# Two mixed attention and expert layers on one core: a new order of expert steps, and results added one step later

## The chip, the cores and the metric

One Trainium2 chip, of which the program uses 1 core. The metric is the device time of one launch in microseconds. The time before is the median of three runs, 1272.5 us (1272.12, 1276.44 and 1272.5).

## The reference, cut to what matters

Two layers run over 256 tokens of width 1024 (128 context tokens and 128 latent ones). Each layer is a block of three kinds of attention, an output projection `w_out`, and then a layer of 64 experts, six for each token, plus one shared expert. The change touches the expert layer only:

```python
def swiglu(x, wg, wu, wd):
    return (silu(x @ wg) * (x @ wu)) @ wd            # 1024 -> 256 -> 1024

def moe_ffn(h, p):                                   # 256 tokens
    xf = h.reshape(T, D)
    top_idx, top_w = route(xf, p['router_w'], p['router_bias'])   # 6 experts of 64
    ...
    yb = lax.map(expert_block, (xb, block_e))        # swiglu with the weights of expert e
    routed = segment_sum(yb[dest] * w_s[:, None], tok_s, num_segments=T)
    shared = swiglu(xf, p['sh_w_gate'], p['sh_w_up'], p['sh_w_down'])
    return (routed + shared).reshape(B, N, D)
```

All weights are f32. Each expert has three matrices (gate, up, down) of 1024 KB, so a layer reads 192 of them from memory once.

How many tokens an expert gets depends on the data. With the inputs of this case, the busiest experts among the 58 that are ranked (below) have 74, 47, 41, 41, 39, 39, 38, 35, 35, 34, 34, 32, 32, 29, ... tokens in layer 0 and 67, 47, 47, 40, 39, 37, 36, 35, 33, 33, 33, 32, 32, 30, ... in layer 1. The six experts that are not ranked have at most 33.

## The kernel before, in words

**Units and steps.** An expert's work is a unit. Units 0 to 5 are the experts 0 to 5 (static: their weights can be fetched before the router has run); the other 58 experts are ranked by their token counts once routing is known, and unit u is the expert of that rank. A step works on 128 slots of tokens: kind S is one unit with 128 slots, D is two units of 64, Q is four units of 32. `ORDER` (line 46) gives each step's kind and first unit. It has 21 steps, numbered from 0. After step 9 (`LOOP = 10`) comes a step in a loop, a D that works on two more units (62 and 63, which are the experts of ranks 18 and 19, ahead of the lighter ones) and, if an expert has more tokens than its unit has slots, on further ones: the loop runs `again` times, at least once. So a layer has 22 steps when nothing overflows. `AGAIN` is the first unit of the loop.

**A step on TensorE** (`step`, with the helpers inside it):
- gate products (L1387, with b = 6) and up products (L1387, b = 7), 64 each at most, from the gathered tokens `xg`;
- the gather for the next step (L1330, twice 16 products: tokens `h2` times the 0/1 matrix `pick`), and between its halves four transposes (L1400, L1402);
- down products (L1420, two halves of 8);
- adding (L1352, 16 products): the step's result `ysb`, spread back to the tokens by the weights `sa`, is added to `xview` in PSUM. It comes right behind the down products whose result it needs.

In the last step there is no gather, and between gate and up stand five products on constants (L1364, warm-up). Its down loads come as halves.

VectorE builds `pick` (`choose`) and `pickw` (`weigh`), copies the first half of each gather and each down result; ScalarE copies the second halves. A semaphore count of a gather is G, of a step J; with an extra gather behind the loop (the loop's last pass has gathered for a pass that does not come) G is J plus a correction.

**Which unit is which.** `slots_by_expert` (L1267, four transposes) and `slots_by_unit` (L1274, four products) turn the positions and weights of the tokens from the order of experts into that of units. Before, they stand inside step 0, and step 1's up products wait for the result (`units`), though step 1 itself is static.

**The weights' way in.** Every weight load is issued by SyncE, in one queue, in the order of the table `LOADS`: loads n = 0 to 191 a layer, 1024 KB each (and one for the shared expert's down matrix). First the 18 loads of the three static steps, then, step by step, gate, up, down. On chip they go into 19 chunks: 12 of a ring, and `attn`, `attn_w`, two of `spare`, `mixed`, `ht` and `wide`, which serve other work in the attention part. `chunk_places` says which load goes to which chunk and which earlier load it replaces. SyncE waits until the products that use the earlier load are through: for a gate load's chunk until that step's gate products (`gl`), up (`gu`), down (`y1`). Since the queue is in order, a load that waits holds back all behind it.

The first loads of the dynamic steps, before: load 18 waits for the router (`plan`), 19 and 20 for step 0's gate products, 21 and 22 for its up, 23 and 24 for its down; 25 and 26 for step 1's gate, 27 and 28 for its up, 29 and 30 for its down. Loads 18 to 29 are those of the step with units 18 to 21 (step 2), 30 to 41 of that with 22 to 25 (step 4). Load 31 waits for step 2's gate products.

During the output projection the ring chunks 6 to 11 hold `w_out`, in two slots of 6144 columns of which it uses 4096. All of chunks 6 to 11 are handed out only once `w_out` has been used (`y_mm`, L1159).

```python
                    if p == 6:
                        sp.wait_ge(S["y_mm"], KD * (l + 1))
...
                                sp.wait_ge(S[used_by[part]], x + ((x + 15) >> 4) + (done + LOOP - 1))
...
                pe.wait_ge(S["xga"], done + (LOOP + l + 1))
                pe.wait_ge(S["xgb"], done + (LOOP + l + 1))
                for _ in gather(done + (LOOP + l + 1)):
                    pass
```

## Time and profile before

| | |
|---|---|
| median of three runs | 1272.5 us (1272.12 to 1276.44) |
| profiled execution, its own time | 1273.4 us |
| its span | 1271.6 us |
| mean granted TensorE clock | 0.987 |
| TensorE busy | 1209.9 us (95%) |
| VectorE busy | 310.4 us (24%) |
| ScalarE busy | 192.9 us (15%) |
| DMA traffic | 495.00 MB, mean 389 GB/s |
| expert steps of layer 0 | from about 182 to 640 us |
| expert steps of layer 1 | from about 800 to 1258 us |

The rows further down come from this one profiled execution. Times are microseconds from the start of the span. Engines: PE is TensorE, PEld its weight loads, DVE VectorE, ACT ScalarE, SP SyncE, and a q behind a name is that engine's sequencer, which issues DMAs. A line number is that of the kernel before. "out<-in" names the buffers; in a line with a wait, `<-` names what ended it. PEclk is the granted TensorE clock as a share of full speed, and the DMA share is the mean busy share of the 16 DMA engines, which the view can put a little above 1.

### The profile page before, as it was taken

What the parts mean: (1) busy time and instruction counts of PE and PEld (TensorE: products, weight loads), DVE (VectorE), ACT (ScalarE), POOL (GpSimd) and SP (SyncE); (2) the same over time, 40 slices, a digit from 0 to 9 for tenths busy, and PEclk for the clock granted to TensorE, in tenths of its full rate; (3) what the DMA queues carried; (4) which work ended last, traced back from release to release, by engine and by line L of the source; (5) the groups of instructions that cost most, each with busy time, mean ns of one, the idle gap of its engine ahead of it and who ended that gap; (6) DMA issues with size and microseconds to landing.
All of it is one profiled execution on the core that took longest, in us unless ns stands there. A gap on an engine that the chain in (4) does not pass through costs nothing.

```text
span 1271.6 us, 22858 instructions
## 1 busy us (share of the span) xinstructions
PE 1209.9 (95%) x9511; PEld 800.5 (63%) x9511; DVE 310.4 (24%) x883; ACT 192.9 (15%) x471; POOL 37.7 (3%) x73
## 2 busy tenths in 40 slices
PE   8999999999999999988899999999999999999795
PEld 4445876666577767655554567766566776775563
DVE  2057341213111111111130764221311121111112
ACT  1125221100111011100010442011011010110011
POOL 2210000000000000000020100000000000000000
PEclk9999999999999999998999999999999999999899
DMA  9999998999999999999996896999999999999995
GB/s 369 389 388 404 407 368 344 383 419 420 421 421 421 420 420 420 421 399 420 409 372 248 328 369 248 350 358 420 420 421 421 420 420 421 421 421 408 421 421 203
DMA packets 86630, 495.00 MB, mean 389 GB/s; under 512 B 11948, under 2 KB 18016, under 8 KB 33024
## 3 DMA queue, kind: packets, MB, share of 16 engines
q1 hardware_dynamic: 83744, 488.38, 94.7%
q0 software_dynamic: 2240, 4.64, 1.1%
q8 instruction: 76, 1.25, 0.4%
q10 hardware_dynamic: 544, 0.52, 0.1%
q14 instruction: 26, 0.21, 0.0%
HBM read 491.20 MB, written 2.50 MB: 388 GB/s over the span
## 4 chain that ended last, share of the span: by engine, by line
PE 58%; issue 24%; DMA 9%; DVE 4%; SPq 3%; ACT 1%; POOL 0%; POOLq 0%; ACTq 0%; DVEq 0%
PE ps L1387 14%; PE ps L931 7%; PE ps L1330 7%; PE ps L1420 6%; PE ps L1352 6%; PE ps L1159 4%; DMA ring<-in_exp_w_up 4%; DMA ring<-in_exp_w_down 4%; PE ps L898 3%; PE ps L1283 2%; SPq L655 2%; SPq L650 1%; PE ps L1116 1%; DMA ring<-in_w_ada 1%; DMA mixed<-in_exp_w_down 1%
## 5 line engine op out<-in xcount | busy, mean ns | idle before, releaser
L1387 PE MATMUL ps<-ring,kt_buf 128*32 128x256 f32 (+2 forms) x3200 | 307.9, 390 | 24.6 <-DMA ring<-in_exp_w_up 15.5
L1387 PEld LDWEIGHTS ps<-ring,kt_buf 128*32 128x32 f32 (+2 forms) x3200 | 190.0, 123 | 121.0 <-issue 45.4
L1330 PE MATMUL ps<-kt_buf,attn 128*128 128x128 f32 x1472 | 185.9, 280 | 1.8 <-DVE kt_buf L2016 1.8
L1330 PEld LDWEIGHTS ps<-kt_buf,attn 128*128 128x128 f32 x1472 | 174.9, 194 | 17.0 <-issue 14.3
L1352 PE MATMUL ps<-kt_buf 128*128 128x256 f32 x704 | 163.8, 385 | 3.2 <-DVE kt_buf L2134 1.8
L1352 PEld LDWEIGHTS ps<-kt_buf 128*128 128x128 f32 x704 | 130.3, 190 | 56.2 <-issue 22.7
L1420 PE MATMUL ps<-ring,kt_buf 128*32 128x512 f32 (+1 forms) x544 | 135.3, 611 | 2.7 <-DMA ring<-in_exp_w_down 2.7
L931 PE MATMUL ps<-ring,ht 128*128 128x456 f32 x256 | 98.9, 547 | 0.6 <-DVE ht L1694 0.6
L2122 DVE SCALAR_TENSOR_TENSOR kt_buf<-kt_buf,ps 128x256 f32<-128x256 f32 x44 | 18.5, 421 | 325.3 <-ACT kt_buf L1619 325.3
L931 PEld LDWEIGHTS ps<-ring,ht 128*128 128x128 f32 x256 | 48.3, 190 | 50.4 <-issue 48.2
L1621 ACT ACTIVATE kt_buf<-ps 128x512 f32<-128x512 f32 x44 | 26.3, 597 | 288.0 <-PE ps L1402 288.0
L2134 DVE COPY kt_buf<-ps 128x512 f32<-128x512 f32 x44 | 30.4, 692 | 141.0 <-PE ps L1420 141.0
L1159 PE MATMUL ps<-ht,ring 128*128 128x256 f32 x256 | 58.7, 382 | 0.0
L1420 PEld LDWEIGHTS ps<-ring,kt_buf 128*32 128x32 f32 (+1 forms) x544 | 34.6, 120 | 37.3 <-issue 34.8
L1619 ACT ACTIVATE kt_buf<-ps 128x256 f32<-128x256 f32 x44 | 16.9, 385 | 270.5 <-PE ps L1387 270.5
L2125 DVE TENSOR_TENSOR kt_buf<-kt_buf,ps 128x256 f32<-128x256 f32 x44 | 18.5, 421 | 153.9 <-PE ps L1387 153.9
L1420 PE MATMUL ps<-attn_w,kt_buf 128*32 128x512 f32 (+2 forms) x112 | 52.2, 597 | 1.9 <-ACT kt_buf L1621 1.4
L2051 DVE COPY kt_buf<-ps 128x512 f32<-128x512 f32 x46 | 31.8, 691 | 86.2 <-PE ps L1330 86.2
L1387 PE MATMUL ps<-spare,kt_buf 128*32 128x256 f32 (+1 forms) x448 | 52.6, 389 | 0.0
L1420 PE MATMUL ps<-attn,kt_buf 128*32 128x512 f32 (+2 forms) x112 | 51.9, 597 | 0.5 <-DMA spare<-in_exp_w_down 0.5
L1159 PEld LDWEIGHTS ps<-ht,ring 128*128 128x128 f32 x256 | 47.4, 190 | 6.1 <-issue 0.3
L1630 ACT ACTIVATE kt_buf<-ps 128x512 f32<-128x512 f32 x44 | 26.3, 597 | 147.7 <-PE ps L1420 147.7
(307 smaller groups left out, 1158.2 us busy)
## 6 DMA issues: line engine op xcount, KB each, us to landing
ring<-in_exp_w_up SPq DMA_DIRECT2D x104, 1024.0 KB, 22.7
ring<-in_exp_w_gate SPq DMA_DIRECT2D x96, 1024.0 KB, 21.0
ring<-in_exp_w_down SPq DMA_DIRECT2D x68, 1024.0 KB, 19.6
ring<-in_w_ada SPq DMA_DIRECT2D x10, 3072.0 KB, 14.1
spare<-in_exp_w_up SPq DMA_DIRECT2D x16, 1024.0 KB, 26.8
spare<-in_exp_w_down SPq DMA_DIRECT2D x16, 1024.0 KB, 26.7
attn<-in_exp_w_down SPq DMA_DIRECT2D x14, 1024.0 KB, 21.3
spare<-in_exp_w_gate SPq DMA_DIRECT2D x12, 1024.0 KB, 8.9
```

What stands on the lines that cost most here:

```text
L655: sp.dma_start(down_of(c)[:, :, h * 512:(h + 1) * 512], I["exp_w_down"][l, e, :, h * 512:(h + 1) * 512].rearrange("(p k) n -> p k n", p=P) ...
L898: last = pe.matmul(ps[32 * q:32 * q + 32, 7, :], csilu[:, k, :], ring[:, slots[l][ent], o:o + 512], start=(k in (0, apart)), stop=(k in (a ...
L931: return pe.matmul(ps[:, 4 * t + n, 0:NZ], ht[:, k, t * T:(t + 1) * T], rows_of(l, i)[:, k - WIN_K[i][0], o:o + NZ], start=(k == 0), stop= ...
L1159: last = pe.matmul(ps[:, Y_BANK[c % 4], (c // 4) * 256:(c // 4) * 256 + 256], w, ht[:, k, :], start=(k == 0), stop=(k == KD - 1))
L1330: last = pe.matmul(ps[:, 4 + b, (c % 4) * P:(c % 4 + 1) * P], h2[:, t, c * P:(c + 1) * P], pick[:, t, :], start=(t == 0), stop=(t == NG - 1))
L1352: last = pe.matmul(xview[:, c, :], ysb[:, c * P:(c + 1) * P], sa[:, 0:NG * T], start=(i == 0 and c % 2 == 0), stop=True, skip_group_check= ...
L1387: last = pe.matmul(ps[w * e:w * (e + 1), b, 0:DE], xg[:, k, w * e:w * (e + 1)], half_of(chunk_of(l, load_of(part, i, e)))[:, k, :], start= ...
L1420: last = pe.matmul(ps[w * e:w * (e + 1), 4 + b, :], sa[:, 256 + k * P + w * e:256 + k * P + w * (e + 1)], down_of(chunk_of(l, load_of("dow ...
L1621: act.activation(sa[:], ps[:, 7, :], ACT.Copy).then_inc(S["sa"], 1)
L1630: act.activation(ysb[:, 512:1024], ps[:, 5, :], ACT.Copy).then_inc(S["yb"], 1)
L2051: dve.tensor_copy(xg[:, 0:4, :].rearrange("p a b -> p (a b)"), ps[:, 4, :]).then_inc(S["xga"], 1)
L2134: dve.tensor_copy(ysb[:, 0:512], ps[:, 4, :]).then_inc(S["ya"], 1)
```

## The change

1. **Adding is put off by a step.** The adding products for step J - 1 now stand in step J, behind its up products; in the last step between the gate products and the warm-up. The last step's own result is added at its end as before. Step 0 adds nothing, step 1 opens the accumulation.
2. **Early assignment.** `slots_by_expert` and `slots_by_unit` move ahead of step 0, into the gathers for it. They use the PSUM banks 0 and 1 now, and ScalarE and not VectorE copies `by_expert`.
3. **Two fixed chunks beside w_out.** Chunks 8 and 11, the third ones of the two slots, which `w_out` does not use, are handed out before the rest of 6 to 11, so two loads more are issued before the wait for `y_mm`.
4. **Useful last gather of the loop.** VectorE writes the first units of step 10 behind the loop's last units, so the last gather of the loop is step 10's. The gather behind the loop is gone, and G equals J everywhere.
5. **20 steps and the loop's** in place of 21 and the loop's, and a new order. A new kind T has three units (64, 32, 32 slots). One D and one S step are gone and one T step has come; there are 11 Q steps as before. The first dynamic step, Q18, is step 1. The loop's units 62 and 63 are now the ranks 16 and 17, and units 16 and 17, with T's 32 slots, hold the ranks 18 and 19; unit 7, which had 128 slots, has 64.
6. Room for 34 further units in place of 32, and constants that nothing reads are dropped.

```diff
-FEW = {"S": 1, "D": 2, "Q": 4}
-SLOTS = {"S": 128, "D": 64, "Q": 32}
+SLOTS = {"S": (128,), "D": (64, 64), "T": (64, 32, 32), "Q": (32, 32, 32, 32)}
+FEW = {kind: len(slots) for kind, slots in SLOTS.items()}
-ORDER = (("D", 0), ("D", 2), ("Q", 18), ("D", 4), ("Q", 22), ("Q", 26), ("D", 8), ("Q", 30), ("S", 6), ("Q", 34),
-         ("Q", 38), ("D", 10), ("Q", 42), ("D", 12), ("S", 7), ("Q", 46), ("D", 14), ("Q", 50), ("Q", 54), ("D", 16), ("Q", 58))
+ORDER = (("D", 0), ("Q", 18), ("D", 2), ("Q", 22), ("D", 4), ("Q", 26), ("Q", 30), ("S", 6), ("Q", 34), ("D", 7),
+         ("D", 9), ("Q", 38), ("Q", 42), ("Q", 46), ("Q", 50), ("Q", 54), ("D", 11), ("T", 15), ("D", 13), ("Q", 58))
...
+BESIDE_OUT = (8, 11)
...
-    opened = [SPARE_C, SPARE_C + 1] + list(range(6)) + [ATTN_C, ATTN_W_C, MIXED_C] + list(range(6, RCH)) + [HT_C, WIDE_C]
+    opened = [SPARE_C, SPARE_C + 1] + list(range(6)) + [ATTN_C, ATTN_W_C, MIXED_C] + list(BESIDE_OUT) \
+        + [c for c in range(6, RCH) if c not in BESIDE_OUT] + [HT_C, WIDE_C]
...
-                                sp.wait_ge(S[used_by[part]], x + ((x + 15) >> 4) + (done + LOOP - 1))
+                                sp.wait_ge(S[used_by[part]], x + ((x + 31) >> 5) + (done + LOOP - 1))
...
-                    def add(b):
+                    def add(b, of, signal=False):
 
-                        pe.wait_ge(S["ya" if b == 0 else "yb"], J + 1)
+                        pe.wait_ge(S["ya" if b == 0 else "yb"], of)
                         for c in range(4 * b, 4 * b + 4):
                             last = pe.matmul(xview[:, c, :], ysb[:, c * P:(c + 1) * P], sa[:, 0:NG * T],
-                                             start=(i == 0 and c % 2 == 0), stop=True, skip_group_check=True)
+                                             start=(i == 1 and c % 2 == 0), stop=True, skip_group_check=True)
...
+                    def add_step_before():
+
+                        add(0, J)
+                        add(1, J)
...
                         if end and b == 7:
+                            add_step_before()
 
                             for _ in range(WARM_LAST):
                                 pe.matmul(ps[:, 7, :], ident, tbl[:, 0:512], start=True, stop=True)
...
                         last.then_inc(S[signal], 1)
+                    if i and not end:
+                        add_step_before()
                     if i == SHARED[2]:
                         shared_down()
...
-                    if i == 0:
-                        slots_by_expert()
...
                         if end:
-                            add(b)
-                    if not end:
-                        add(0)
-                        add(1)
+                            add(b, J + 1, signal=True)
+                    if i == 0:
+                        pe.wait_ge(S["units"], l + 1)
 
                 pe.wait_ge(S["h2"], 2 * l + 2)
-                g = gather(done + l)
+                g = gather(done)
                 next(g)
                 next(g)
                 order_experts()
+                slots_by_expert()
                 next(g)
                 list_experts()
+                slots_by_unit()
...
-                pe.wait_ge(S["xga"], done + (LOOP + l + 1))
-                pe.wait_ge(S["xgb"], done + (LOOP + l + 1))
-                for _ in gather(done + (LOOP + l + 1)):
-                    pass
                 for i in range(LOOP, STEPS):
-                    step(done + i, done + (i + l + 1), ORDER[i][0], i, end=(i == STEPS - 1))
+                    step(done + i, ORDER[i][0], i, end=(i == STEPS - 1))
...
                 again = dve.value_load(xpairs[0:1, 0:1], min_val=1, max_val=XP_MAX)
+                after = bass.ds(2 * again + AGAIN, FEW["D"])
+                first = slice(ORDER[LOOP][1], ORDER[LOOP][1] + FEW["D"])
+                dve.tensor_copy(posu[:, :, after], posu[:, :, first])
+                then(dve.tensor_copy(wu[:, :, after], wu[:, :, first]))
```

How instructions stand on an engine is shown in the next fences: a line number, the operation, out<-in and the shape, how many in a row, and which semaphore the first one waits for.

SyncE in layer 0, from the fourth gate load of the step with units 18 to 21 on, before (a `TENSOR_LOAD` of `xexp` reads the expert's number for a gate load):

```order
L735 TENSOR_LOAD xexp [waits s_gu]
L735 ISA x2
L650 ISA
L650 DMA ring<-in_exp_w_gate 128x2048
L650 DMA ring<-in_exp_w_up 128x2048
L650 DMA ring<-in_exp_w_up 128x2048 [waits s_y1]
L650 DMA ring<-in_exp_w_up 128x2048
L650 DMA ring<-in_exp_w_up 128x2048 [waits s_gl]
L650 DMA ring<-in_exp_w_down 128x2048
L650 DMA attn<-in_exp_w_down 128x2048 [waits s_gu]
L650 DMA attn_w<-in_exp_w_down 128x2048
L650 DMA ring<-in_exp_w_down 128x2048 [waits s_y1]
```

The same place after:

```order
L650 DMA ring<-in_exp_w_gate 128x2048
L650 DMA ring<-in_exp_w_up 128x2048
L650 DMA ring<-in_exp_w_up 128x2048 [waits s_y1]
L650 DMA ring<-in_exp_w_up 128x2048
L650 DMA ring<-in_exp_w_up 128x2048 [waits s_gl]
L650 DMA spare<-in_exp_w_down 128x2048 x2
L650 DMA ring<-in_exp_w_down 128x2048 [waits s_gu]
L650 DMA ring<-in_exp_w_down 128x2048
L735 TENSOR_LOAD xexp [waits s_gu]
```

The rows are loads 21 to 29, then 30. Before, the wait for `s_gl` ahead of load 25 is for the gate products of step 1, which is static and for which these loads are not. After, step 1 is the step that these loads are for: load 25 (its fourth up matrix) waits for its own gate products, 26 and 27 likewise, 28 and 29 for its own up products, and load 32 for its own down products.

TensorE in layer 0 from the end of step 0's second gather half to the next gate products, before:

```order
L1330 MATMUL ps<-kt_buf,attn 128x128 x8
L1420 MATMUL ps<-ring,kt_buf 64x512 x4
L1274 MATMUL ps<-attn_w,ada_sb 128x64 x4
L1420 MATMUL ps<-ring,kt_buf 64x512 x4
L1352 MATMUL ps<-kt_buf 128x256 x8
L1387 MATMUL ps<-ring,kt_buf 64x256 x16
```

After, what stands ahead of step 0's gate products (from the order of experts on):

```order
L1267 MATMUL ps<-tbl,mixed 64x128 x2
L1267 MATMUL ps<-tbl,kvg 64x128 x2
L1330 MATMUL ps<-kt_buf,attn 128x128 x8
L1260 MATMUL ps<-attn_w,tbl 1x64
L1274 MATMUL ps<-attn_w,ada_sb 128x64 x4
L1391 MATMUL ps<-spare,kt_buf 64x256 x16
```

After, step 1 from its up products to its first down products:

```order
L1391 MATMUL ps<-ring,kt_buf 32x256 x33
L1352 MATMUL ps<-kt_buf 128x256 x8
L1330 MATMUL ps<-kt_buf,attn 128x128 x8
L1406 MATMUL ps<-tbl,kt_buf 128x128 x2
L1408 MATMUL ps<-tbl,kt_buf 128x128 x2
L1330 MATMUL ps<-kt_buf,attn 128x128 x8
L1424 MATMUL ps<-spare,kt_buf 32x512 x2
```

The products L1267 and L1274 have left step 0, step 0's down products are followed by step 1's gate products, and adding (L1352) stands between step 1's up products and the gather.

TensorE around the last step's gate products, before:

```order
L1402 MATMUL ps<-tbl,kt_buf 128x128 x2
L1330 MATMUL ps<-kt_buf,attn 128x128 x8
L1420 MATMUL ps<-ring,kt_buf 64x512 x8
L1352 MATMUL ps<-kt_buf 128x256 x8
L1387 MATMUL ps<-ring,kt_buf 32x256 x32
L1364 MATMUL ps<-tbl 128x512 x5
L1387 MATMUL ps<-ring,kt_buf 32x256 x3
```

After:

```order
L1408 MATMUL ps<-tbl,kt_buf 128x128 x2
L1330 MATMUL ps<-kt_buf,attn 128x128 x8
L1424 MATMUL ps<-ring,kt_buf 64x512 x8
L1391 MATMUL ps<-ring,kt_buf 32x256 x32
L1352 MATMUL ps<-kt_buf 128x256 x8
L1370 MATMUL ps<-tbl 128x512 x5
L1391 MATMUL ps<-ring,kt_buf 32x256 x3
```

Adding has moved from ahead of the last gate products to between them and the warm-up products (L1364 before, L1370 after).

## Rows read from the trace of the kernel before

**Rows 1.** The page: slices of traffic (each 31.8 us), and its DMA issues (median us to landing)

```profile
GB/s 369 389 388 404 407 368 344 383 419 420 421 421 421 420 420 420 421 399 420 409 372 248 328 369 248 350 358 420 420 421 421 420 420 421 421 421 408 421 421 203
...
ring<-in_exp_w_up SPq DMA_DIRECT2D x104, 1024.0 KB, 22.7
```

**Rows 2.** Windows: stretch, us, busy PE, PEld, DVE, ACT, POOL, PEclk, DMA share, GB/s

```profile
182.00:240.00 58.00, 58.00 (x496) 38.86 (x496) 14.09 (x43) 7.13 (x13) 0.00 (x0) 1.00 0.90 348
240.00:546.00 306.00, 303.66 (x2573) 207.65 (x2573) 54.74 (x129) 34.78 (x65) 0.00 (x0) 1.00 1.01 420
546.00:640.00 94.00, 78.62 (x739) 48.59 (x738) 12.03 (x28) 7.51 (x14) 0.00 (x0) 0.95 1.00 409
776.00:784.00 8.00, 8.00 (x44) 7.17 (x44) 3.17 (x12) 0.83 (x2) 0.00 (x0) 1.00 0.00 0
802.00:857.00 55.00, 55.00 (x471) 37.08 (x468) 12.18 (x35) 6.53 (x12) 0.00 (x0) 1.00 0.89 343
```

**Rows 3.** Waits of SyncE's DMA queue: waited for, total us, times, longest

```profile
SPq L561 <- PE ps L1387: 263.3, 53, 23.4
...
SPq L650 <- PE ps L1159: 33.5, 2, 22.1
```

**Rows 4.** Chain of waits, 182 to 240 us: start, us, what

```profile
182.34 7.06 PE ps L1387 x64
...
191.84 0.44 PE ps L1267 x4
...
195.93 1.03 PE ps L1274 x8
...
198.83 3.65 PE ps L1352 x16
202.48 7.06 PE ps L1387 x64
209.53 1.98 PE ps L1330 x16
...
213.75 3.58 PE ps L1420 x16
...
220.99 7.04 PE ps L1387 x128
```

**Rows 5.** Timeline of SyncE's DMA issues: load 23, and load 31

```profile
199.00 0.33 SPq L650 DMA_DIRECT2D ring<-in_exp_w_up  x1
...
225.42 0.34 SPq L650 DMA_DIRECT2D ring<-in_exp_w_gate  x1
```

**Rows 6.** DMA issues (median us to landing): loads 23/24, 31, and 23/24 of layer 1

```profile
ring<-in_exp_w_up SPq DMA_DIRECT2D x2, 1024.0 KB, 6.3
...
ring<-in_exp_w_gate SPq DMA_DIRECT2D x1, 1024.0 KB, 4.8
...
ring<-in_exp_w_up SPq DMA_DIRECT2D x2, 1024.0 KB, 8.5
```

**Rows 7.** Windows for line L1387 alone: PE, PEld, PEclk, DMA share, GB/s

```profile
575.00:581.00 6.00, 0.00 (x0) 0.00 (x0) 0.90 1.01 416
581.00:588.00 7.00, 6.31 (x64) 3.18 (x64) 0.60 1.02 425
1200.00:1206.00 6.00, 5.35 (x64) 3.30 (x64) 0.72 1.02 426
```

**Rows 8.** Timeline of TensorE, layer 1, last steps: start, us, operation [idle before]

```profile
1210.28 0.59 PE L1420 MATMUL ps<-attn,kt_buf 128*32 128x512 f32 x1 [0.48 <-DMA spare<-in_exp_w_down]
...
1236.02 3.66 PE L1387 MATMUL ps<-ring,kt_buf 128*32 128x256 f32 x64
1239.61 4.56 PE L1364 MATMUL ps<-tbl 128*128 128x512 f32 x10
...
1246.50 0.42 PE L1387 MATMUL ps<-ring,kt_buf 128*32 128x256 f32 x3 [2.33 <-DMA attn<-in_exp_w_up]
...
1257.14 0.59 PE L1420 MATMUL ps<-attn_w,kt_buf 128*32 128x512 f32 x1 [0.15 <-DMA mixed<-in_exp_w_down]
```

More of the change, by code:

```diff
@@ L1334, in gather, with step @@
                         yield
-                def step(J, G, kind, i, extra=None, end=False):
-                    w = SLOTS[kind]
+                def step(J, kind, i, extra=None, end=False):
+                    slots_of = [slice(sum(SLOTS[kind][:e]), sum(SLOTS[kind][:e + 1])) for e in range(FEW[kind])]
                     def wait_for(part):
@@ L1612, in copy_second, with step @@
                         .then_inc(S["xgb"], 1)
-                def step(J, G, shared=None, end=False):
+                def step(J, shared=None, end=False):
                     act.wait_ge(S["gl"], J + 1)
@@ L1641, in _ @@
                         shared_tanh(SHARED.index(i))
-                        step(done + i, done + (i + l), shared=SHARED.index(i))
+                        step(done + i, shared=SHARED.index(i))
                     else:
-                        step(done + i, done + (i + l))
+                        step(done + i)
                 act.wait_ge(S["more"], l + 1)
@@ new lines, in of_units @@
+                def of_units(table, u, few):
+                    return table[:, :, u:u + few] if isinstance(u, int) else table[:, :, bass.ds(u, few)]
+                def choose(kind, u):
+                    for first, few, w, at in equal_slots(kind):
+                        last = dve.tensor_tensor(pick[:, :, at].rearrange("p t (e s) -> p t e s", e=few),
+                                                 tbl[:, C_SLOT:C_SLOT + w].unsqueeze(1).unsqueeze(1)
+                                                 .to_broadcast([P, NG, few, w]),
+                                                 of_units(posu, u + first, few).unsqueeze(3)
+                                                 .to_broadcast([P, NG, few, w]), ALU.is_equal)
+                    last.then_inc(S["sel"], 1)
@@ L2030, in _ @@
+                    last.then_inc(S["sw"], 1)
                 choose(*ORDER[0])
```

137 lines of the change are left out of this document (58 added, 79 removed).

## The prediction

> **What bounds the kernel now.** I read the page's slices first, then the stage windows, then SP's waits, then the chain of waits through the first expert steps, and last the timelines of the last step. In the slices the traffic stands at 420 GB/s through the middle of both expert phases [rows 1], and the stage windows put a number on it: 420 GB/s at a DMA share of 1.01 for 306 us of layer 0, against 348 GB/s and 0.90 in the 58 us ahead of it, and 343 GB/s and 0.89 at the same place of layer 1 [rows 2]. One load is 1024 KB; at 420 GB/s that is 2.50 us, and the 192 expert loads and the shared one of a layer are 193 x 2.50 = 482 us. TensorE looks as full as the queue (58.00 of 58.00 us, 303.66 of 306.00), but in the last 94 us it is busy for 78.62 us only while the traffic stays at 409 [rows 2]. So TensorE runs ahead and then waits at the end of each layer for data. The queue is the bound, and it loses time only where it has nothing to do: at the start of the expert phase, where 18 loads lie ready and each further one waits until TensorE has used up a chunk (SP waits 263.3 us in 53 waits for the gate and up products, [rows 3]).
>
> I split the change by what it can do to two things: the moment from which the queue never runs dry again, and what stands between the last landing and the end.
>
> **The step that goes, and the extra gather: no gain of their own.** A step is 220.99 - 202.48 = 18.51 us of TensorE whatever it holds: gate and up 7.06, gather and transposes 213.75 - 209.53 = 4.22, down 3.58, adding 3.65 [rows 4]. One step a layer goes (18.5 us) and the gather behind the loop, twice 1.98. These 22.5 us lie in the 306 us in which the queue is saturated, and the bytes stay the same. The cover is the load that is still on its way: 22.7 us from issue to landing in the median [rows 1]. If that cover were not there (TensorE the true bound), it would be a gain of 22.5 us a layer, which is a rival below. Whether a unit overflows depends on the counts: the first expert on 32 slots is now that of rank 18 (the thirteenth of the ranked ones), and with 32 tokens in both layers it just fits, so the loop still runs once, as before.
>
> **Two loads ahead of w_out's end: nothing.** In layer 1 the queue is idle at 776 to 784 (0 GB/s, [rows 2]) while SP waits for the w_out products (33.5 us in two waits, [rows 3]). Two loads, 5 us, now fill this. But they are of step 2, the queue has caught up with all 18 before step 0 is over, and it then runs dry anyway waiting for chunks. The bounds: nothing, or 5 us a layer if the queue never ran dry behind it; the share of 0.89 behind it [rows 2] decides for nothing.
>
> **The new start: Q18 as step 1.** Layer 0 of the trace, moved by hand:
> - The products that assign slots (0.44 and 1.03 us, [rows 4]) now stand ahead of step 0's gate and not inside step 0: the gate starts 1.47 later, the down products still end at 198.83. With adding put off, step 1's gate starts there and ends at 202.4.
> - Loads 23 and 24 wait for step 0's down products as before: issued at 199.00, landed after 6.3 us in the mean of the two [rows 5, 6], the second at 206.7.
> - Load 25 now waits for step 1's own gate, is behind them in the queue and lands at 206.7 + 2.5 = 209.2. Step 1's up products need it: TensorE stands idle for 6.8 us, where it had no wait at all.
> - After such a wait, 6 us in this trace, the granted clock was 0.60 over the window of the next 64 products and they took 6.31 us instead of the 3.66 that they take at full clock [rows 7, 8]; that is a stretch at 1.2 of 2.4 GHz. So up ends at 215.5, and not 212.8.
> - Adding 3.65, gather and transposes 4.22, down 3.58: step 1 ends at 227.0. Loads 28 and 29, issued at 215.8, land at 220.6 and 223.1 (4.8 us for a load into an empty queue, [rows 6]) and are just in time.
> - Load 32 waits for these down products. Load 31 of the trace was issued 0.9 behind its release (the gate half of the products that start at 220.99 ends at 224.5, the issue is at 225.42, [rows 4, 5]); with the same 0.9 it is 227.9, landing 232.7. It is the last that starts into a dry queue.
> - Before, the last dry one is load 31, issued at 225.42 [rows 5], landing 230.2; load 32 behind it lands at 232.7 at the earliest. So the start gives 0 in layer 0.
> - In layer 1 the two loads behind step 0's down products took 8.5 us and not 6.3 [rows 6]. Before, this had slack; now load 25 hangs on it, so 2.2 us are lost there. I take half, 1.1, since the stretch behind it before was not free of the same delay.
> Bounds for the start: with the full clock in the up products 2.65 a layer better, that is 5.3 - 1.1 = 4.2 us gained; at worst, with the full 2.2 and as much again in layer 0, 4.4 us lost. I take 1 us lost, since the 6.31 comes from a wait of the same length.
>
> The Trainium skill (TensorE: Matmul & The Clock Gate, "HAM oscillation — how this bites in real kernels") says that waits for DMA send the array back to its slow clock, so that each burst behind one starts cold. The trace agrees (6.31 against 3.66, [rows 7, 8]); without the rule the start would come out 5.3 us better over two layers. The same skill (DMA: Bandwidth & Descriptors, "Anatomy of one DMA — SWDGE (gpsimd) path") fits one DMA as 2.0 us plus bytes over 436 GB/s, an estimate of 4.4 us for ours; the trace has 4.8 [rows 6] and decides; by the page the start would be 0.4 a layer better.
>
> **The middle.** Steps 9, the loop's and 10 are now three pair steps in a row: TensorE needs 18.5 for each, the queue 15.0, so 10.5 us of the queue's lead go. Of the 22.7 us [rows 1] 12 are left, over the 4.8 that a load needs: nothing.
>
> **The last step.** Adding for the step before moves from ahead of the last gate to behind it, ahead of the five warm-up products. Layer 1, before: down 1210.28 (after a wait for its load), two addings, one pair step, gate 1236.02, warm-up 1239.61 for 4.56, ends 1244.17, and the up products wait 2.33 more, until 1246.50, for their load [rows 8]. The step with that down is now T15. Its up loads land three loads (7.5 us) ahead of its down load, at 1202.8, and between the two TensorE must now do up 3.53, adding 3.65 and gather 4.22, 11.4 us: down starts at 1214.2, 3.9 late. Then down 3.58, gate and up 7.06, adding 3.65, gather 4.22, down 3.58: 1236.3; gate 3.6, adding 3.65, warm-up 4.56: 1248.1. The up load is there at 1246.5, so up starts 1.6 late. The last down half waits for its own load by only 0.15 us at 1257.14 [rows 8], so 1.45 of this shows at the end of the layer. With layer 0 the same: 3 us lost. Bounds: 0 (the clock or the copies give it back) and 3.9 x 2 = 7.8 us (nothing hides it).
>
> **The sum**: start 1 lost, last steps 3 lost, step, gather, early loads and middle 0: 4 us slower, less 1.5 us for small gaps in the traffic of the last 94 us, which a TensorE that uses up its chunks earlier can close (409 GB/s against 420 there is 2.5 us a layer at most, [rows 2]; of both layers' 5 I take a third). Net +2.5. The profiled execution took 1273.4 us (span 1271.6), so 1275.9 there; the runs' median is 0.9 lower: 1275.
>
> **The rivals.**
> - *The early four-expert step pays.* If the clock does not fall in step 1 and the last step's lateness is absorbed, the start's 4.2 and the gaps' 2.5 remain: 1266. For it: half the price rests on one wait's clock. Against: 6.31 us after 6 us idle, and 5.35 after a shorter one at 1200 us [rows 7].
> - *TensorE is the bound*, as its busy time and SP's 263.3 us of waits for it suggest: 22.5 us a layer, 1228. Against: the queue stands at its top rate all that time.
> - *The starved start (slower).* Step 1 is the place: four gates, four ups and four downs with 19 chunks held by steps 0, 2 and 4. If loads 23 to 25 take 8.5 us in both layers and the down products wait too for load 29, each layer's dry queue lasts 3 us longer, and every later pair step runs 3 us nearer to it; with the last steps at 3.9 each the sum is 6 + 7.8 less 3 = 11 slower: 1283. It decides from a step 1 that ends over 3 us later than 227.0.
> - *A unit overflows*, because a near tie in routing falls the other way on the chip: one more pass of the loop, 6 loads of 2.50, 15 us a layer: 1290 to 1305.
>
> **How the numbers follow.** Forecast 0.44; early step pays 0.28, half of it beyond 0.5%; TensorE the bound 0.07; starved start 0.18, most of it beyond 0.5%; overflow 0.03. A measurement of this kernel tells 0.5% (6.4 us) from no change. Faster: 0.14 + 0.07 and a little of the forecast, 0.23. Slower: 0.14 + 0.03, 0.17. Same: 0.60. The range holds the forecast and most of the cases on both sides: 1262 to 1284. The forecast's own is 1270 to 1280.
>
> **What would show it.** Right, if in the new trace step 1's up products start after 6 to 7 us of idle time named after a DMA, at a clock of about a half; the queue's last dry moment is at 226 to 229; the traffic is 420 through the middle; TensorE's idle time in a layer's expert steps grows by some 22 us, what it no longer has to do; and the last up products start with no idle time ahead of them, behind the warm-up. Wrong, if the steps stay free of waits to the end and the middle gets shorter, if step 1 has no wait, or if the loop runs twice.

## The result and the profile after

The changed kernel takes 1312.7 us in the median of four runs (1311.19 to 1316.54), the kernel before 1272.3 us beside it: a ratio of 1.0317, 95% interval 1.030 to 1.0335. It is 40 us slower; 1275 us were forecast, with a range up to 1284. The profiled execution took 1311.2 us, its span is 1309.4 us, 37.8 us more than before. In both traces layer 0 ends where the products of line 875 begin: 642.8 us before, 661.7 us after. That is 18.9 us, and the second layer loses the other half.

The page of the changed kernel, the slices of traffic and the DMA issues (as in [rows 1]):

```profile
GB/s 370 390 384 410 408 360 332 418 419 420 421 395 405 373 421 421 421 420 422 410 195 242 334 371 290 321 352 419 420 422 415 410 374 409 420 422 420 421 405 42
...
ring<-in_exp_w_up SPq DMA_DIRECT2D x96, 1024.0 KB, 17.3
```

The windows of the changed kernel, with the columns of [rows 2], a window in the middle (427 to 450 us), and then the T step and the pair step D13 by themselves:

```profile
182.00:240.00 58.00, 48.87 (x439) 33.77 (x439) 9.79 (x26) 5.24 (x10) 0.00 (x0) 0.94 0.88 337
240.00:546.00 306.00, 278.55 (x2491) 184.90 (x2489) 51.39 (x132) 31.51 (x60) 0.00 (x0) 0.96 1.00 411
427.00:450.00 23.00, 23.00 (x231) 15.63 (x228) 3.52 (x8) 2.18 (x4) 0.00 (x0) 1.00 0.87 353
546.00:640.00 94.00, 91.62 (x653) 53.53 (x654) 11.36 (x25) 8.71 (x16) 0.00 (x0) 0.97 1.02 417
583.30:616.90 33.60, 33.60 (x174) 13.73 (x171) 2.89 (x6) 2.18 (x4) 0.00 (x0) 1.00 1.01 421
616.90:635.20 18.30, 18.30 (x134) 12.71 (x132) 2.56 (x5) 2.18 (x4) 0.00 (x0) 1.00 1.02 406
```

The middle window of the kernel before:

```profile
427.00:450.00 23.00, 23.00 (x177) 15.02 (x178) 4.30 (x10) 3.28 (x6) 0.00 (x0) 1.00 1.01 419
```

Two things stand out. In the middle of layer 0 the queue is not full any more: 353 GB/s for 23 us in which TensorE is busy all the time (the kernel before has 419 there). And at the end TensorE, which waited for 15 us of the 94 before, is busy for 91.62 of them: the T step (the one with units 15 to 17) takes 33.6 us of it, the pair step behind it (D13, units 13 and 14) 18.3, at the same full clock.

The timeline of TensorE in the changed kernel, step 1 and then the shared expert's products ahead of step 6 (start, us, operation, idle time before):

```profile
198.79 0.38 PE L1391 MATMUL ps<-wide,kt_buf 128*32 128x256 f32 x1 [1.51 <-DMA ring<-in_exp_w_gate]
...
210.07 5.19 PE L1391 MATMUL ps<-ring,kt_buf 128*32 128x256 f32 x64 [7.62 <-DMA ring<-in_exp_w_up]
...
307.60 9.39 PE L1283 MATMUL ps<-heads,ht 128*128 128x512 f32 x16 [4.91 <-DVE ht L1694]
```

The same products in the kernel before:

```profile
299.57 7.10 PE L1283 MATMUL ps<-heads,ht 128*128 128x512 f32 x16 [1.26 <-DVE ht L1694]
```

The start came as forecast: 7.6 us idle ahead of step 1's up products. The last line was not in the forecast: TensorE waits 4.9 us for VectorE there and not 1.3, and the products take 2.3 us longer, at a granted clock of 0.75 in their window and not 1.00.

The chain of waits of the changed kernel at the end of layer 0 (start, us, what):

```profile
554.96 13.39 DMA ring<-in_exp_w_up
...
568.48 3.67 PE ps L1391 x32
...
579.83 3.58 PE ps L1424 x16
583.42 17.96 PE ps L1391 x96
601.37 3.65 PE ps L1352 x16
...
609.05 7.94 PE ps L1424 x24
616.99 7.06 PE ps L1391 x64
...
635.30 3.59 PE ps L1391 x64
638.89 3.65 PE ps L1352 x16
642.54 4.29 PE ps L1370 x10
646.84 3.63 PE ps L1391 x64
```

From 568.48 to 650.47 the chain is TensorE alone, 82 us. The last half load of the layer was issued at 626.99 before the change and at 630.78 after it, and landed 11.2 and 11.3 us later:

```profile
626.99 1.03 SPq L655 DMA_DIRECT2D mixed<-in_exp_w_down  x1
mixed<-in_exp_w_down SPq DMA_DIRECT2D x1, 512.0 KB, 11.2
...
630.78 1.04 SPq L655 DMA_DIRECT2D mixed<-in_exp_w_down  x1
mixed<-in_exp_w_down SPq DMA_DIRECT2D x1, 512.0 KB, 11.3
```

So the last landing was at 638.2 with the layer's end 4.6 us behind it, and is now at 642.0 with the end 19.6 us behind it. Of the 18.9 us, the last landing is 3.8 later, and the end stands 15 further behind it. In the chain the T step's gate and up products are 17.96 us where a pair step's are 7.06, and its down products 7.94 where they are 3.58: 15.3 us too many.

TensorE's weight loads in the T step (same columns):

```profile
583.77 0.14 PEld L1391 LDWEIGHTS ps<-ring,kt_buf 128*32 128x32 f32 x4 [0.39 <-issue]
584.33 0.19 PEld L1391 LDWEIGHTS ps<-ring,kt_buf 128*64 128x64 f32 x2 [0.41 <-issue]
584.90 0.14 PEld L1391 LDWEIGHTS ps<-ring,kt_buf 128*32 128x32 f32 x4 [0.39 <-issue]
```

A product leaves two records here (one k, an eighth of the 1024 inputs, is four products in eight records in a Q step). Each k of the T step runs as two groups, the 64-slot product and the two of 32 slots, 0.565 us apart, so 1.13 us for a k. A pair or four products of one width take 0.441 us (7.06 us for the 16 k of gate and up). Nothing of the narrow group lies beside the wide one.

### The profile page after: what moved, and what is told of

The parts are those of the page before. It is cut to its first block, busy times and chain, and to the rows that moved or that the text cites. A ratio compares the mean times of both kernels' runs of the same rounds, so it can differ in the third digit from the quotient of the medians.

```text
span 1309.4 us, 22476 instructions
## 1 busy us (share of the span) xinstructions
PE 1203.0 (92%) x9343; PEld 772.5 (59%) x9343; DVE 301.5 (23%) x871; ACT 188.5 (14%) x463; POOL 37.8 (3%) x73
## 3 DMA queue, kind: packets, MB, share of 16 engines
HBM read 491.17 MB, written 2.50 MB: 377 GB/s over the span
## 4 chain that ended last, share of the span: by engine, by line
PE 60%; issue 24%; DMA 8%; DVE 4%; SPq 2%; ACT 1%; POOL 0%; POOLq 0%; ACTq 0%; DVEq 0%
PE ps L1391 15%; PE ps L931 7%; PE ps L1352 7%; PE ps L1330 7%; PE ps L1424 7%; PE ps L1159 4%; DMA ring<-in_exp_w_up 4%; PE ps L898 3%; PE ps L1283 3%; DMA attn<-in_exp_w_up 2%; SPq L650 1%; DMA ring<-in_exp_w_gate 1%; PE ps L1116 1%; DMA ring<-in_w_ada 1%; PE ps L1141 1%
## 5 line engine op out<-in xcount | busy, mean ns | idle before, releaser
L1391 PE MATMUL ps<-ring,kt_buf 128*32 128x256 f32 (+2 forms) x3040 | 320.7, 405 | 27.6 <-DMA ring<-in_exp_w_up 16.7
L1391 PEld LDWEIGHTS ps<-ring,kt_buf 128*32 128x32 f32 (+2 forms) x3040 | 171.7, 124 | 131.4 <-issue 80.3
L1330 PE MATMUL ps<-kt_buf,attn 128*128 128x128 f32 x1344 | 164.1, 275 | 1.8 <-DVE kt_buf L2025 1.8
L1330 PEld LDWEIGHTS ps<-kt_buf,attn 128*128 128x128 f32 x1344 | 160.1, 192 | 4.7 <-ACT attn L1604 1.0
L1352 PE MATMUL ps<-kt_buf 128*128 128x256 f32 x672 | 156.6, 386 | 3.2 <-DVE kt_buf L2138 1.8
L1352 PEld LDWEIGHTS ps<-kt_buf 128*128 128x128 f32 x672 | 124.2, 190 | 37.3 <-issue 15.3
L1391 PE MATMUL ps<-spare,kt_buf 128*32 128x256 f32 (+2 forms) x512 | 84.3, 391 | 17.3 <-DMA ring<-in_exp_w_up 12.6
L1391 PEld LDWEIGHTS ps<-spare,kt_buf 128*32 128x32 f32 (+2 forms) x512 | 45.4, 124 | 40.0 <-issue 27.4
L1391 PE MATMUL ps<-mixed,kt_buf 128*32 128x256 f32 (+1 forms) x160 | 43.2, 432 | 18.1 <-DMA ring<-in_exp_w_up 12.6
L1391 PE MATMUL ps<-attn,kt_buf 128*32 128x256 f32 (+1 forms) x192 | 49.5, 402 | 0.0
```

Of the source, the lines that this page charges most:

```text
L1330: last = pe.matmul(ps[:, 4 + b, (c % 4) * P:(c % 4 + 1) * P], h2[:, t, c * P:(c + 1) * P], pick[:, t, :], start=(t == 0), stop=(t == NG - 1))
L1352: last = pe.matmul(xview[:, c, :], ysb[:, c * P:(c + 1) * P], sa[:, 0:NG * T], start=(i == 1 and c % 2 == 0), stop=True, skip_group_check= ...
L1391: last = pe.matmul(ps[slots_of[e], b, 0:DE], xg[:, k, slots_of[e]], half_of(chunk_of(l, load_of(part, i, e)))[:, k, :], start=(k == 0), st ...
```

## The experiments

All ran beside the kernel before, in four sets: t_four to t_four_cover, defer_only to tail, no_warm to no_cover, and the last three. The medians of the kernel before were 1273.2, 1272.3, 1273.0 and 1271.2 us in these sets, so 1 or 2 us between kernels of different sets mean nothing; the ratios, with 95% intervals, compare better.

**t_four.** The T step's 64-slot unit as two products of 32 slots from the same chunk.

```diff
...
+                    if kind == "T":
+                        slots_of = [(0, slice(0, 32)), (0, slice(32, 64)), (1, slice(64, 96)), (2, slice(96, 128))]
...
-                            for e in range(FEW[kind]):
-                                last = pe.matmul(ps[slots_of[e], b, 0:DE], xg[:, k, slots_of[e]],
+                            for e, at in slots_of:
+                                last = pe.matmul(ps[at, b, 0:DE], xg[:, k, at],
```

> The changed kernel (1312.7 us), with the three-unit step's 64-slot unit worked as two products of 32 slots from the same chunk, so that the step issues four products of 32 at a time like a Q step. Theory A (the mixed widths 64, 32, 32 make the T step slow, and the end of each layer hangs on TensorE): gate and up of the T step fall from 18.1 to about 7.1 us, down from 7.9 to 3.6, the step from 33.6 to 18.3; 15.3 us a layer, 1282 us. Rival B (the loss comes from the order of the last steps and from a queue that ran dry in the middle; the T step's length is hidden behind loads): within 5 us of the changed kernel, 1308 to 1312. Rival C (the granted clock, 0.97 against 0.987, is the cause): the T step stays long.

Measured: 1289.7 us (ratio 1.0131, 1.010 to 1.0162), 23 us less. The timeline of its T step:

```profile
584.78 3.66 PE L1393 MATMUL ps<-ring,kt_buf 128*32 128x256 f32 x64
590.71 0.65 PE L1393 MATMUL ps<-ring,kt_buf 128*32 128x256 f32 x3 [2.27 <-DMA attn<-in_exp_w_up]
```

The window of its up products, for their line alone (columns as in [rows 7]):

```profile
590.71:595.92 5.21, 5.21 (x64) 2.71 (x64) 0.68 1.00 415
```

The gate products take 3.66 us. Behind them TensorE now waits 2.27 us for a load, and the up products take 5.21 us at a clock of 0.68. With the 3.66 of full clock, that is 3.8 us lost in layer 0; in layer 1 the wait is 1.33 us and the clock full. So 5.1 of the 7.6 us that are missing between the 23 that came back and 30.6 are seen, and the rest is open. Rivals B and C fall: same order, same clock (0.966), 23 us less.

**t_apart.** The T step's products with the 64-slot unit first for all k, then the two others; the down products likewise.

```diff
+                        runs = ((0,), (1, 2)) if kind == "T" else (range(FEW[kind]),)
-                        for k in range(KD):
+                        for k, few in [(k, few) for few in runs for k in range(KD)]:
...
-                            for e in range(FEW[kind]):
+                            for e in few:
```

> The changed kernel (1312.7 us), with the T step's products in two runs: the 64-slot unit for all k first, then the two 32-slot units for all k. If the T step loses both by the lack of overlap between the two widths and by each switch of width (now at each k): gate and up fall from 18.1 to 14.2 us (4 runs of 8 at 0.445 each), down from 7.9 to 7.3, so 4.5 us a layer and 1304 us. If only the lack of overlap counts and a switch is free: no change, 1312. If only the alternation is at fault and the widths overlap: 18.1 to 7.1 and 1282.

Measured: 1306.2 us (1.0256, 1.0239 to 1.0274), 6.5 us less. The gate and up products of the T step as a window for their line alone (columns as in [rows 7]), first of this kernel:

```profile
585.41:599.78 14.37, 14.37 (x96) 7.72 (x95) 1.00 1.02 423
```

and of the changed kernel:

```profile
583.25:601.37 18.12, 18.12 (x96) 5.30 (x95) 1.00 1.01 421
```

32 groups at 0.441 us are 14.1 us, nearly all that is left when each width runs by itself. So two things make up the loss. Each k has two groups and not one, 7.1 us. And a change of width costs time: the edit takes away 28 of the 31 changes and 3.75 us (18.12 less 14.37), 0.13 us each, about what the start times say (0.565 less 0.441). That the widths don't overlap while they alternate is read from those start times; t_apart keeps them apart and can't show it.

**cover.** The adding for step 5 ahead of the shared products of step 6.

```diff
+                    if i == SHARED[0]:
+                        add_step_before()
+                        shared_gate_up(0)
                     pe.wait_ge(S["xga"], J + 1)
...
-                    if i and not end:
+                    if i and not end and i != SHARED[0]:
                         add_step_before()
```

> The changed kernel (1312.7 us), with the adding for step 5 put back ahead of step 6's shared gate and up products (elsewhere it stays put off). Before the change it filled the time in which VectorE prepares the shared expert's input; after, TensorE waits 4.9 us there (1.3 before) and the shared products take 9.4 us at a lower clock (7.1 before). Theory D (this wait puts TensorE behind, and the queue runs dry at 429 to 448 us for some 5 us): wait and slow clock go, 5.9 us of TensorE a layer, and with the dry queue up to 5 us a layer of the total: 1302 to 1307. Rival (the wait is hidden since the queue is full): 1311 to 1313.

Measured: 1303.8 us (1.0235, 1.0211 to 1.0259), 9 us less, within theory D's range. TensorE waits 1.26 us ahead of the shared products again, and they take 7.11 us. The window from 427 to 450 us carries more:

```profile
311.19 7.11 PE L1283 MATMUL ps<-heads,ht 128*128 128x512 f32 x16 [1.26 <-DVE ht L1697]
...
427.00:450.00 23.00, 23.00 (x224) 16.13 (x221) 3.31 (x7) 2.17 (x4) 0.00 (x0) 1.00 0.98 399
```

399 GB/s against 353, with no other edit: TensorE's lateness had kept chunks from the queue.

**t_four_cover.** Both edits.

> Both: the T step as four products of 32, and the adding for step 5 ahead of the shared products. If the two causes add (15.3 and some 5 us a layer): 1272, as before the change. If the T step alone sets the end: 1282, as with that edit alone. If, with the T step mended, the last landing sets the end: between these, 1275 to 1280, and the last up products of a layer wait for a load again.

Measured: 1277.3 us (1.0035, 1.0026 to 1.0045): 35 us less than the changed kernel, 12.3 less than t_four. The time is that of the third expectation, but its sign is missing: the last up products of layer 0 start with no wait for a load. Layer 0 ends at 642.75 us, as before the change (642.81).

**defer_only.** The kernel before, with the adding put off and nothing else.

```diff
+                            add(0, J)
+                            add(1, J)
 
                             for _ in range(WARM_LAST):
...
+                    if i and not end:
+                        add(0, J)
+                        add(1, J)
...
-                    if not end:
-                        add(0)
-                        add(1)
```

> The kernel before (1272.5 us) with one part of the change alone: the adding of a step's result put off into the next step (in the last step ahead of the warm-up products), and at the gather behind the loop a wait for the copies that the adding used to wait for. Theory D (put off, the adding no longer covers the time in which the shared expert's input is prepared; TensorE waits about 5 us and the clock falls): the wait ahead of the shared products of step 6 grows from 1.3 to about 5 us, these take 9.4 and not 7.1 us, but as the queue does not run dry in the middle of this kernel, only the last step's 1.5 us a layer show: 1275 us. If TensorE sets the middle here too: 6 us a layer more, 1284. Rival (putting off is free or a gain): 1272 or less.

Measured: 1273.5 us (1.0013, 1.0004 to 1.0023). The wait ahead of the shared products is 4.91 us and they take 9.62, and yet the kernel loses only 0.5 to 3 us by the interval. So the wait is hidden here.

**old_order.** The changed kernel with the table of steps of before. (Its step 10 is a Q step, while the loop's last gather is laid out for a pair step. So of step 10's four experts one gets its tokens, one gets those of another expert, and two get none. The instructions are those of a Q step in number and shape.)

> The changed kernel (1312.7 us) with the order of the steps of before (21 steps, no T step) and all else of the change kept. Theory (the order with its T step and its run of pair steps made the loss): within 5 us of before, 1272 to 1277. Rival (adding put off, early assignment or the loop's useful gather cost much of it): over 1285.

Measured: 1269.5 us (0.9977, 0.9967 to 0.9987). The order, with the T step in it, makes the whole loss: without it 1312.7 becomes 1269.5 us.

**old_start.** t_four_cover with the first steps D0, D2, Q18, D4, Q22.

> The changed kernel with the T step as four products and the adding for step 5 ahead of the shared products (1277.3 us), and with the first five steps in the order of before (D0, D2, Q18, D4, Q22). Theory E (the four-unit step as step 1 starves TensorE for 6 to 7 us in each layer and leaves the queue dry 2 us longer): last dry load lands at about 230 and not 232 us, step 1 has no wait, 2 to 3 us a layer less: 1272. Rival (the early four-unit step is no loss, since the end of a layer hangs on TensorE's chain behind the last four-unit step but one): 1277 to 1280, the wait only comes later.

Measured: 1270.8 us (0.9984, 0.9974 to 0.9994), 6.5 us less than t_four_cover. The last load of the start that lands behind a dry queue is load 29 at 223.3 us and not load 32 at 232.0. I had expected 230. With the adding put off, step 2's gate products come sooner, and load 31, which waits for them, is issued at 220.25 and not 225.42 [rows 5]; the queue is not dry then. defer_only issues it at 222.15, so most of this is the put-off adding, which the early Q step had hidden.

```profile
220.25 0.34 SPq L650 DMA_DIRECT2D ring<-in_exp_w_gate  x1
```

**tail.** t_four_cover with the end Q46, D11, Q50, T15, Q54, D13, Q58.

> The changed kernel with the T step as four products and the adding for step 5 ahead of the shared products (1277.3 us), and with the small steps at the end dealt out between the four-unit steps: ... Q46, D11, Q50, T15, Q54, D13, Q58. Theory F (with D11, T15, D13 in a row TensorE is 1 to 3 us late at the end, 10.6 to 11.5 us behind the last landing and more): the last up products wait for their load again, and the layer ends about 10 us behind the last landing: 1 to 2 us a layer less, 1274. Rival (the queue sets the end and each layer ends as before): 1277.

Measured: 1277.9 us (1.0053, 1.0036 to 1.007), no change from t_four_cover. Theory F falls: where the T step costs no more than a pair step, dealing out the small steps brings nothing.

**no_warm.** old_start with `WARM_LAST = 0`.

> The kernel old_start (1270.8 us) without the five warm-up products ahead of the last up products. Its trace has no wait ahead of these products: the chain adding (3.7), warm-up (4.5), up is later than the load, and layer 0 ends 11.8 us behind its last landing, where the kernel before ended 10.0 us behind it. Theory G (TensorE's chain sets the end of each layer there): 1.8 us a layer less, until the last landing sets the end: 1267. Rival (without the warm-up the products behind run at half clock): 1271 or more.

Measured: 1269.4 us (0.9972, 0.9959 to 0.9985), 1.4 us under old_start's value, with intervals that overlap, so no gain is shown. In the timeline the last up products wait for their load once more:

```profile
624.73 0.42 PE L1396 MATMUL ps<-ring,kt_buf 128*32 128x256 f32 x3 [3.01 <-DMA attn<-in_exp_w_up]
...
624.73:628.39 3.66, 3.66 (x64) 2.35 (x64) 1.00 1.05 384
```

The second line is their window (columns as in [rows 7]): 3.66 us at a clock of 1.00 behind 3.01 us of waiting and no warm-up, so the rival's half clock did not come. Theory G has some support: layer 0 ends 4.6 us behind the last landing and in old_start 6.3. (The expectation's 11.8 and 10.0 us run from the first half of the last load and not from its second, which lands last.)

**no_beside.** old_start with `BESIDE_OUT = ()`.

> The kernel old_start (1270.8 us) with chunks 8 and 11 handed out after w_out, as before the change. The prediction's claim (the two early loads bring nothing, since the queue runs dry later all the same): 1270.8. Rival (they end the queue's static loads 3.5 us earlier in layer 1, and the loads of the first dynamic step with them): up to 3.5 us more, 1274.

Measured: 1270.7 us (0.9985, 0.9972 to 0.9997). Against old_start's 0.9984 the two early loads bring nothing.

**order21.** The 21 steps of before with D10 ahead of Q38, the adding for step 5 ahead of the shared products, and all else of the change.

> All of the change but its order of steps: the 21 steps of before, with D10 moved ahead of Q38 since the loop's last gather serves a pair step, and the adding for step 5 ahead of the shared products. Compared with old_start (1270.8 us, 20 steps with the T step as four products): the claim that a step less brings nothing of its own, since the queue sets the middle: 1269 to 1272. Rival (a step less is worth its TensorE time, 18.5 us a layer, or part of it): over 1275.

Measured: 1269.1 us (0.9967, 0.9956 to 0.9977). With 18.5 us more TensorE work a layer than old_start it is no slower. It is also 0.3% faster than the kernel before, and which part of the change brings that was not taken apart.

**no_cover.** old_start with the adding for step 5 put off as in the change.

> The kernel old_start (1270.8 us) with the adding for step 5 put off as in the change. TensorE waits 4.9 us ahead of the shared products again and runs them at a lower clock: 5.9 us a layer. Theory H (the lead that the queue has in the middle decides what this costs; with the early four-unit step it was 6 us a layer: 1289.7 against 1277.3): with the old start the queue's last dry moment is 9 us earlier, so it may stay filled: 1271 to 1276. Rival (the wait always costs its full length): 1282.

Measured: 1270.5 us (0.9983, 0.9973 to 0.9994). The wait of 4.91 us is in the trace, and the time is old_start's: it costs nothing here.

**start_alone.** The changed kernel with only the start in the old order.

> The changed kernel (1312.7 us) with only the first five steps in the order of before; the T step and the adding as in the change. Theory (in the changed kernel three things act: the T step 15.3 us a layer behind the last four-unit step but one, and a queue that runs dry in the middle since both the early four-unit step and the uncovered wait have used up its lead; with the old start the lead holds and only the T step is left): 15.3 us a layer over no_cover (1270.5), 1301; the queue has no dry stretch between 400 and 450 us. Rival (the early four-unit step costs only its own 3 us a layer, as it did with the two other edits): 1306.

Measured: 1298.6 us (1.0211, 1.0196 to 1.0225), 14.1 us less than the changed kernel and 28.1 more than no_cover, which differs from it in the T step alone. (By the ratios, which take out that the two ran in different sets, it is 29 us.) The shared products and the middle window of this kernel:

```profile
298.66 9.66 PE L1283 MATMUL ps<-heads,ht 128*128 128x512 f32 x16 [4.91 <-DVE ht L1694]
...
427.00:450.00 23.00, 23.00 (x240) 14.77 (x243) 4.48 (x10) 3.37 (x6) 0.00 (x0) 1.00 1.01 414
```

TensorE comes to the shared products at 298.66 and not at 307.60, 9 us sooner with the same steps behind it, and the queue stays full.

**t_between.** old_start's order and adding, with the T step's mixed widths as in the change, and the end dealt out as in tail.

> The kernel old_start (1270.8 us) with the T step's three products as in the change (mixed widths), but the small steps dealt out between four-unit steps: Q46, D11, Q50, T15, Q54, D13, Q58. The open point: is the T step's 15.3 us always paid, or only where TensorE has no waits behind it? Theory (between four-unit steps TensorE waits about 10 us for loads behind it, so that much is hidden): 5 us a layer, 1281. If always paid: 1301. If fully hidden: 1271 to 1273.

Measured: 1269.0 us (0.9983, 0.9974 to 0.9992). All of the 15.3 us a layer is hidden, more than I expected. The T step is as slow as ever:

```profile
541.75:559.90 18.15, 18.15 (x96) 5.33 (x96) 1.00 0.99 411
```

From 560 to 600 us TensorE waits for loads for 0.21 us in all, where the kernel before has one wait of 6.26 us among others:

```profile
581.22 6.31 PE L1387 MATMUL ps<-ring,kt_buf 128*32 128x256 f32 x64 [6.26 <-DMA ring<-in_exp_w_up]
```

So the T step fills time in which TensorE would have waited for the next loads.

**best21.** order21 with `WARM_LAST = 0`.

> order21 (1269.1 us) without the five warm-up products, which no_warm showed to hold up the end by about 1 us: 1267.5. Rival (with its waits closer to the end the products run at half clock without the warm-up): 1270.

Measured: 1267.9 us (0.9975, 0.9963 to 0.9986). The lowest median of all kernels here, 0.25% under the kernel before beside it; by the ratio order21 (0.9967) is lower, and which of them or of t_between is best is not settled by these intervals.

## Why the prediction was wrong

**The T step.** The prediction's main error stands in its second step, "A step is ... 18.51 us of TensorE whatever it holds". I read this from a D step and carried it over to a kind that the trace of before does not have. D, Q and S do agree in it, since each issues products of one width. The T step mixes two: 33.6 us. I gave this no bound from the other side, though the unit's products one after the other would have been one. It is 28.1 us of the 40 (start_alone less no_cover), close to twice 15.3. The rest is the early Q step with the put-off adding (14.1 us, below), less some 2 us that the rest of the change gains (no_cover).

That it shows in full hangs on the order. D11, T15 and D13 stand in a row: 21 loads, 52.5 us of the queue by the prediction's 2.50, while TensorE needs 18.3 + 33.6 + 18.3 = 70 us. So TensorE sets the end. The rival "TensorE is the bound" did not come true as it was put (order21, with a step more a layer, is no slower than old_start), but I had asked only what a shorter TensorE would bring and not what a longer one would cost. t_between shows the same step between Q steps for nothing.

The Trainium skill has the rule that I should have weighed (TensorEngine Tiling (Array Packing), "Key Properties"): changing the tiling mode, and not just the tile, drains TensorE. It gives no price. t_apart agrees, with 0.13 us for each change. The larger part here is that products of two widths don't overlap while they alternate; whether that and the price of a change are one mechanism the runs don't show.

**The middle: "nothing".** Wrong too. I subtracted 10.5 us for three pair steps from a lead of 22.7 us (how long a load is under way behind others in the queue). That was the median over the whole kernel and not the lead at that place. One load there, issued at 423 us, first of the kernel before, then of the changed one, and one of the changed kernel issued at 442 us (time to landing at the end of each line):

```profile
ring<-in_exp_w_gate SPq DMA_DIRECT2D x1, 1024.0 KB, 14.7
...
ring<-in_exp_w_down SPq DMA_DIRECT2D x1, 1024.0 KB, 6.4
...
ring<-in_exp_w_gate SPq DMA_DIRECT2D x1, 1024.0 KB, 5.8
```

5.8 us is 1 us above the 4.8 of a load into an empty queue [rows 6]. I also left out what the adding had covered: now TensorE waits 4.9 and not 1.3 us ahead of step 6, and the products behind take 2.3 us more, 5.9 us of TensorE in all. With the late start the queue ran dry. Which edit gets the blame depends on what else is there: the early four-unit step costs 14.1 us in all (changed kernel less start_alone), 6.5 with the two other causes mended (t_four_cover less old_start); the missing cover costs 12.3 with the early start (t_four less t_four_cover) and nothing with the old one (no_cover). Both draw on one thing, the queue's lead: with the old start it is there (15.2 us for the load issued at 423 us in start_alone), and the missing cover costs nothing. The end of layer 0 shows the two causes apart: in start_alone the last landing is at 635.4, 6.6 us earlier than in the changed kernel, and the end still stands 20.0 behind it; so the start and the cover move the landing, the T step the distance behind. What the runs don't settle is how these 14.1 us divide between the dry stretch of the start and that of the middle.

**The new start, as such, came out well.** Forecast for layer 0: the second of loads 23 and 24 at 206.7, load 25 at 209.2, up from there after 6.8 us idle, step 1's end at 227.0, load 32 landed at 232.7. Measured: 206.7, 209.9, up at 210.07 after 7.6 us, 226.5, 232.3. In layer 1 the wait is 8.6 us. The up products took 5.19 us at a clock of 0.70 (6.30 at 0.57 in layer 1), for 6.31 forecast and 3.66 at full clock. They start cold, as the Trainium skill says of work behind waits for DMA (TensorE: Matmul & The Clock Gate, "HAM oscillation — how this bites in real kernels"). What failed is what I compared it with. "So the start gives 0" was nearly true against the kernel before, where load 32 landed at 233.8; but against the same kernel with the old start the last dry moment is 9 us later (load 32 at 232.0, load 29 at 223.3), and TensorE comes to the shared products 9 us later. Putting off the adding alone gives that much: in defer_only load 29, at 222.9, is the last behind a dry queue.

**The last step.** Forecast: TensorE some 1.6 us late for the last up products, 3 us in all. The order of events was right, adding and warm-up in front of a load that is there already. defer_only, which has little else, loses 0.5 to 3 us; no_warm gives 1.4 us back, inside the noise. In the changed kernel this is hidden behind the T step.

**Step and gather that go, the two early loads: nothing.** Right: order21 against old_start, and no_beside.

**The rivals and the signs.** "The starved start" named a mechanism that was at work (every later pair step runs nearer to a dry queue), with 11 us as its price; but its own sign did not come, since step 1 ended at 226.5 and not 3 us behind 227.0, and it has no term for the T step. (In its price, "6 + 7.8 less 3", the 3 us come from no row.) "The early four-expert step pays" is refuted: the step costs 14.1 us. No unit overflowed: 491.17 MB were read from memory after the change and 491.20 before. Of the signs of being right, the wait and the clock of step 1 and the last dry moment came; the one that failed is the traffic through the middle, 411 GB/s for the 306 us and 353 in its worst part.

## What to carry to other kernels

A new kind of step has to be priced from its products' shapes, not from its siblings: in these traces products of one width lie beside each other, and products of two widths run one after the other and pay for each change. In a kernel that streams its weights, a step's TensorE time is free only as long as the queue's time for the same loads, with the lead that is left, is longer. So put steps that are heavy on TensorE between steps that are heavy on loads, and not in a row ahead of the end. Work that is put off may have covered a wait; before moving it, look at who was waited for behind it, and at the lead the queue has at that very place.

## What the runs showed of the hardware

- A 64-column product and two 32-column products on the remaining columns don't run together when they alternate: 0.565 us a group (changed kernel) against 0.441 for a group in a run of its own width.
- 28 changes of width less save 3.75 us (18.12 in the changed kernel, 14.37 in t_apart), 0.13 us each.
- Two 32-column products from the same chunk, in place of one of 64, cost nothing: the T step's gate products took 3.66 us as four (t_four), the price of a Q step's.
- Of 64 products behind a wait: 3.66 us at a clock of 1.00 behind 3.01 us (no_warm), 5.19 at 0.70 behind 7.62 and 6.30 at 0.57 behind 8.59 (changed kernel).
